# Two block norms of a transformer kernel: four product groups per new tile, and eight kept squares added behind the last low part

## The chip, the cores and the metric

One core of a Trainium2 chip runs the whole program. The metric is the device time of one execution in microseconds (us), median over the runs. Five engines matter: PE (TensorE, matrix products into the eight banks of PSUM), DVE (VectorE), ACT (ScalarE), POOL (GpSimd) and the queue SP, which issues the transfers of weights.

## The reference, cut to what matters

The program is a first block (a mixer of three branches, then a convolutional feed-forward), a second model of two layers (a "fox" attention and a latent attention, each with a feed-forward), on 512 tokens of 1024 channels in float32. The two places that the change touches both have this form:

```
x = x + rmsnorm(y, g_post)          # y: the output projection before it
h = rmsnorm(x, g_pre);  h @ w       # w: ffn_w_up, or the fox projection
rmsnorm(x, g) = x * rsqrt(mean(x*x) + eps) * g
```

## The kernel before

Activations lie transposed, a tile being 128 channels by 512 tokens; 1024 channels are eight tiles (KD = 8). Every float32 product is made of three: high part times high part, high weight times low part, low weight times high part (`split_mm`, lines 596 to 600, and lines 668 to 670 where the tokens stand in the rows). So one tile of one group of 128 output columns is three products, called a triple here. ACT rounds weights and activations to the high part; POOL subtracts and so makes the low part of the weights (WLO, line 590), in pieces of 512 columns, and DVE that of the activations.

The weights come in chunks of 1024 columns through a ring of four slots: SP fetches chunk c when the product groups of chunk c - 4 are done (line 559), ACT casts it (`casts`, line 1203), POOL splits it. `casts(n)` stands at fixed places of ACT's order.

The scale of a norm is not applied before the product but behind it: PE multiplies x times its gain (HH, HL), and DVE multiplies the result by RSTD when it empties the bank. So PE may start on a tile before the sum of squares is known. The sum, SUMSQ, is brought across the partitions by a product with ones (`stats`, line 673, or `stats_in_two`, line 678), and ACT takes the root by Ln and Exp (`root`, line 1219).

The two places are the norm before the first feed-forward (site `ffnpre0`, behind `wout`, here the first norm) and that before the fox attention (site `fox`, behind `down0`, here the second norm). At each:

- ACT squares the projection's tiles (`fb_square`, line 1245), for the last one directly from PSUM, behind `early_table`, which loads the table for Ln.
- PE runs `stats_in_two` and 24 products that are thrown away (`keep_clock(24)`, line 685).
- DVE runs `post_norm` (line 2026). For each tile j: `scaled` (FB times gain and RSTD), `added` (X plus FB), `lo_tile` (HL, once ACT has made HH), and `add_square`, which adds ACT's square to SUMSQ. The loop is written so that tile j+1 is added and j+2 scaled between the low part of j and its square.
- ACT runs for each tile `h_tile` (line 1238): HH, then the square of X into one of two slots of SQ. The square waits until the one two before has been added.
- PE takes the new tiles. First norm (lines 958 to 962): four groups, `gate0.0`, `val0.0`, `gate0.1`, `val0.1` (UP0_HEAD), whose weights share four chunks, two tiles of each group in a chunk. The order is by chunk, then by group, then by the two tiles. `stats` stands in the last chunk behind the second group, so four triples follow it. Second norm (lines 1009 to 1016): four groups of 128 tokens each (`fv0.0` to `fv0.3`), again by chunk, then group, then tile, and `stats` behind all of them; then `foxf`, then `by_token_scale`, which turns RSTD into columns, then `fv1`.

Each PE instruction of these groups waits for the low part of its own tile (`by_tile`). ACT casts the fourth head chunk behind tile 1 at the first norm (line 1430) and behind tile 2 at the second (line 1467), and the chunk after the head behind tile 7 (lines 1431 and 1468), ahead of `root`. Behind `root` it casts `val0.2` (line 1445).

Of the kernel before, what the change touches and what calls it, by code (L numbers as in the profile page):

```python
# [20 lines left out]
ALU = mybir.AluOpType  # L21
ACT = mybir.ActivationFunctionType
# [6 lines left out]
P = 128  # L29
T = 512  # L30
NT = T // P
D = 1024
KD = D // P
# [53 lines left out]
UP0_HEAD = ("gate0.0", "val0.0", "gate0.1", "val0.1")  # L87
# [145 lines left out]
def on_chip_model(nc, xT, weights, params, consts, masks16, masks8, gate_up, pool_w, rope, resets, outT):  # L233
    with ExitStack() as ctx:
# [27 lines left out]
        X = keep("X", [P, KD, T])  # L262
# [7 lines left out]
        SUMSQ = keep("SUMSQ", [P, T])  # L270
# [42 lines left out]
        def over(name, shape, tensor_at, dt=F32):  # L313
            return nc.alloc_sbuf_tensor_at(name, shape, dt, offset=tensor_at)
# [42 lines left out]
        fox = Region(arena)  # L357
# [7 lines left out]
        foh_at = fox.at  # L365
# [4 lines left out]

        FZ = nc.alloc_sbuf_tensor_at("FZ", [P, 2, T], F32, offset=foh_at)
        ONES = nc.alloc_sbuf_tensor_at("ONES", [P, T], F32, offset=foh_at + 2 * T * 4)
        CUMH = over("CUMH", [P, T], foh_at + 3 * T * 4, F32R)
        CUML = over("CUML", [P, T], foh_at + 4 * T * 4, F32R)

# [47 lines left out]
        H = (as_tiles(HH), as_tiles(HL))  # L423
# [15 lines left out]
        lin_done, drained = sem("lin_done"), sem("drained")  # L439

        h_hi, h_lo, sq_done, sumsq, cleared = sem("h_hi"), sem("h_lo"), sem("sq_done"), sem("sumsq"), sem("cleared")
# [64 lines left out]
        def tile(t, j):  # L506

            return t[:, bass.ds(j, 1), :].rearrange("p a n -> p (a n)")
# [86 lines left out]
        def _(pe):  # L595
# [15 lines left out]
            def bank_free(name):  # L611
                if PRIOR[name]:
                    pe.wait_ge(drained, PRIOR[name])

            def part(name, at, hi, lo, ready=None, tiles=None):

                c, first, blocks, col = PARTS[name][at]
                begin, end = tiles or (first, first + blocks)
                if begin == 0:
                    bank_free(name)  # L620
                slot, last = c % RING, at == len(PARTS[name]) - 1
                for k in range(begin, end):
                    n = k - first
                    w = slice(col + n * P, col + (n + 1) * P)
                    weights_ready(c, w.stop)
                    if ready:

                        pe.wait_ge(ready[0], ready[1] + k + 1)
                    mm = split_mm(ps[:, BANK[name], :], WHI[:, slot, w], WLO[:, slot, w], hi[k], lo[k],
                                  k == 0, last and n == blocks - 1)  # L630
                if end == first + blocks:
                    mm.then_inc(lin_done, 1)
# [19 lines left out]
                for at in range(len(PARTS[name])):  # L652
                    part(name, at, hi, lo, ready)

            def token_part(name, at, width, hi, lo, last, rows, ready=None):

                if at == 0:
                    bank_free(name)
                c, first, blocks, col = PARTS[name][at]
                slot, per = c % RING, width // P  # L660
                for n, r in enumerate(rows):
                    o, q = ps[:, BANK[name], n * width:(n + 1) * width], slice(r * P, (r + 1) * P)
                    for m in range(blocks // per):
                        k, w = first // per + m, slice(col + m * width, col + (m + 1) * width)
                        weights_ready(c, w.stop)
                        if ready:
                            pe.wait_ge(ready[0], ready[1] + k + 1)
                        pe.matmul(o, hi[k][:, q], WHI[:, slot, w], start=k == 0, stop=False)  # L668
                        pe.matmul(o, lo[k][:, q], WHI[:, slot, w], start=False, stop=False)  # L669
                        mm = pe.matmul(o, hi[k][:, q], WLO[:, slot, w], start=False, stop=k == last - 1)  # L670
                mm.then_inc(lin_done, 1)

            def stats(site, n):

                pe.wait_ge(sumsq, SQ_AT[site] + n + 2)
                pe.matmul(ps[:, 7, :], ones, SUMSQ[:, :], start=True, stop=True).then_inc(stat_done, 1)
# [16 lines left out]
            def by_tile(site):  # L693
                return h_lo, HH_AT[site]
# [259 lines left out]
            def ffn(f):  # L954
                site = f"ffnpre{f}"
                h = H_OF.get(site, H)
                if f == 0:
                    for at in range(4):
                        for n, name in enumerate(UP0_HEAD):
                            if at == 3 and n == 2:  # L960
                                stats(site, 8)
                            part(name, at, *h, by_tile(site))
                for q in range(0 if f else 2, KF):
                    group(f"gate{f}.{q}", *h, by_tile(site) if q == 0 else None)
                    if q == 0:
                        stats(site, 8)
                    group(f"val{f}.{q}", *h)
                for j in range(KD if f < 2 else KD - 1):
                    group(f"down{f}.{j}", *ACTS[f], (acts, 1 + KF * f) if j == 0 else None)
# [38 lines left out]

            for half in range(2):
                for at in range(NT):  # L1010
                    for r in range(NT):
                        token_part(f"fv{half}.{r}", at, 512, *H, KD, (r,), None if half else by_tile("fox"))
                if half == 0:
                    stats("fox", 8)
                    group("foxf", *H)
                    by_token_scale("fox")
# [183 lines left out]
        def _(act):  # L1200
# [26 lines left out]
            def early_table(func):  # L1227
                warmed[0] += 1
                act.activation(WARM[:, :], con("one"), func).then_inc(warm, 1)
                act.wait_ge(warm, warmed[0])  # L1230

            def square(j, slot, source, site):

                act.wait_ge(sumsq, j + (SQ_AT[site] + 1))
                apart()
                act.activation(SQ[:, slot, :], source, ACT.Square).then_inc(sq_done, 1)  # L1236

            def h_tile(j, slot, gain, site, squares=True):

                apart()  # L1240
                act.activation(H_OF.get(site, H)[0][j], tile(X, j), ACT.Copy, scale=par(gain, j)).then_inc(h_hi, 1)
                if squares:
                    square(j, slot, tile(X, j), site)

            def fb_square(stage, j, site):

                if j < KD - 1:
                    product(f"{stage}.{j}")
                    square(j, j % 2, tile(FB, j), site)
                else:  # L1250
                    early_table(ACT.Ln)
                    act.wait_ge(lin_done, DONE[f"{stage}.{j}"])
                    square(j, j % 2, ps[:, BANK[f"{stage}.{j}"], :], site)

# [170 lines left out]
            root("mixpost", D, RSTD)  # L1425
            for j in range(KD):
                act.wait_ge(x_done, j + 1)
                h_tile(j, j % 2, "ffnpre0", "ffnpre0")
                if j == 1:
                    casts(chunk_of("gate0.0"))  # L1430
            casts(chunk_of("gate0.2"))
# [30 lines left out]
            root("ffnpost", D, RSTD)  # L1462
            for j in range(KD):
                act.wait_ge(x_done, j + (KD + 1))
                h_tile(j, j % 2, "fox", "fox")
                if j == 2:
                    casts(chunk_of("fv0.0"))
            casts(chunk_of("foxf"))
# [198 lines left out]
        def _(dve):  # L1667
# [19 lines left out]
            def add_square(j, slot, site):  # L1687
                dve.wait_ge(sq_done, j + (SQ_AT[site] + 1))

                dve.wait_ge(sumsq, j + (SQ_AT[site] + 2))  # L1690
                dve.tensor_tensor(SUMSQ[:, :], SUMSQ[:, :], SQ[:, slot, :], ALU.add).then_inc(sumsq, 1)  # L1691
# [334 lines left out]
            def post_norm(site, nxt, done):  # L2026

                clear_sum(nxt)
                dve.sem_inc(sumsq, 1)
                scale_known(site)  # L2030

                def scaled(j):
                    stt(tile(FB, j), tile(FB, j), par(site, j), RSTD[:, :], ALU.mult, ALU.mult).then_inc(post_dve, 1)

                def added(j):
                    dve.wait_ge(post_dve, j + (done + 1))
                    dve.tensor_tensor(tile(X, j), tile(X, j), tile(FB, j), ALU.add).then_inc(x_done, 1)

                scaled(0)
                added(0)  # L2040
                scaled(1)
                for j in range(KD):
                    lo_tile(j, nxt, nxt)
                    if j + 1 < KD:
                        added(j + 1)
                    if j + 2 < KD:
                        scaled(j + 2)
                    add_square(j, j % 2, nxt)

            def into_x(stage, site, gain, tiles=KD):  # L2050

# [470 lines left out]
```

## Time and profile before

| | us |
|---|---|
| median of 3 runs | 2198.48 |
| lowest, highest | 2197.4, 2198.51 |
| span of the profiled execution | 2196.6 |

The table holds no time of the profiled execution but its span, from its first to its last instruction; the runs' times also hold what lies around it. Times in rows count from the start of the span. PE's mean granted clock over the span is 0.997 of full speed.

A row of the timeline has an instruction's start and its duration, or, where several alike follow each other, the time that they cover. Consecutive starts tell more than durations, because neighbouring instructions of one engine overlap a little at their ends. The last bracket of a row tells how long the engine was idle before it, and who ended that.

### The profile page before, as it was taken

Reading aid. Unit: us, or ns where it says so; the run is one execution under the profiler, and the core shown is the slowest. Engines: PE = TensorE matmul, PEld = TensorE weight load, DVE = VectorE, ACT = ScalarE, POOL = GpSimd, SP = SyncE. Lnnn points to the kernel's source line nnn. Section 1 sums busy time; section 2 is a strip of 40 time slices with the busy share of each in tenths; the row PEclk is TensorE's granted clock in tenths of the full one; section 3 lists DMA queues with packets and bytes.
Section 4 is the critical chain, followed back from the end, with each engine's and each line's share of the span. In section 5 each row is a group of like instructions: output and inputs, shape, how many; then the busy total and the mean of one; then the engine's idle time right before and its main releaser. Section 6 shows DMA issues by size and latency. Waiting matters only on the chain.

```text
span 2196.6 us, 26113 instructions
## 1 busy us (share of the span) xinstructions
PE 2170.1 (99%) x10388; PEld 1771.0 (81%) x10388; DVE 1201.8 (55%) x1709; ACT 908.1 (41%) x1410; POOL 953.9 (43%) x731
## 2 busy tenths in 40 slices
PE   9999999999999999999999999999999999999998
PEld 6877788878888877777888888887888888888887
DVE  5775324479865126776566661167666425666511
ACT  5224522353443234666533342255544434333323
POOL 5334344545554434321544444544232344544442
PEclk9999999999999999999999999999999999999999
DMA  5222222323333322211333333232111133333332
GB/s 181 78 68 65 75 82 96 106 77 96 96 96 92 98 89 87 68 58 31 114 96 96 96 95 98 95 96 75 56 53 52 60 106 96 96 96 96 94 99 86
DMA packets 58377, 191.76 MB, mean 87 GB/s; under 512 B 6512, under 2 KB 8720, under 8 KB 58256
## 3 DMA queue, kind: packets, MB, share of 16 engines
q1 hardware_dynamic: 58256, 190.09, 27.9%
q8 instruction: 83, 1.36, 0.3%
q14 instruction: 38, 0.31, 0.0%
HBM read 187.96 MB, written 2.10 MB: 87 GB/s over the span
## 4 chain that ended last, share of the span: by engine, by line
PE 92%; DVE 5%; ACT 1%; DMA 1%; issue 1%; SPq 0%; ACTq 0%; POOL 0%; DVEq 0%
PE ps L598 26%; PE ps L600 26%; PE ps L599 26%; PE ps L1111 2%; PE ps L1005 1%; PE ps L668 1%; PE ps L996 1%; PE ps L669 1%; PE ps L670 1%; DMA RAW<-weights 1%; DVE TURNED L1675 1%; PE ps L1060 1%; PE ps L1029 1%; PE ps L726 1%; DVE RT L2264 0%
## 5 line engine op out<-in xcount | busy, mean ns | idle before, releaser
L590 POOL TENSOR_TENSOR WLO<-RAW,WHI 128x512 fp32r<-128x512 f32 (+1 forms) x723 | 951.4, 1342 | 1209.8 <-ACT WHI L1208 1206.7
L1208 ACT ACTIVATE WHI<-RAW 128x1024 fp32r<-128x1024 f32 (+2 forms) x374 | 372.7, 1000 | 661.4 <-DMA RAW<-weights 474.4
L598 PE MATMUL ps<-HH,WHI 128*128 128x512 f32 x1200 | 474.7, 396 | 3.5 <-DVE HL L1678 2.3
L600 PE MATMUL ps<-HH,WLO 128*128 128x512 f32 x1200 | 468.0, 390 | 0.0
L599 PE MATMUL ps<-HL,WHI 128*128 128x512 f32 x1200 | 467.8, 390 | 0.0
L1678 DVE SCALAR_TENSOR_TENSOR CV<-U,PAR,CV 128x512 f32<-128x512 f32 x264 | 287.9, 1109 | 11.2 <-ACT CV L1448 6.1
L598 PEld LDWEIGHTS ps<-HH,WHI 128*128 128x128 f32 x1200 | 225.6, 188 | 57.5 <-issue 5.3
L599 PEld LDWEIGHTS ps<-HL,WHI 128*128 128x128 f32 x1200 | 225.8, 188 | 47.9 <-issue 2.4
L600 PEld LDWEIGHTS ps<-HH,WLO 128*128 128x128 f32 x1200 | 225.6, 188 | 47.6
L598 PE MATMUL ps<-ACTH,WHI 128*128 128x512 f32 (+1 forms) x550 | 209.5, 381 | 0.0
L599 PE MATMUL ps<-ACTL,WHI 128*128 128x512 f32 (+1 forms) x550 | 209.3, 381 | 0.0
L600 PE MATMUL ps<-ACTH,WLO 128*128 128x512 f32 (+1 forms) x550 | 209.3, 381 | 0.0
L1675 DVE TENSOR_TENSOR U<-ps,RSTD 128x512 f32<-128x512 f32 x132 | 89.8, 687 | 209.5 <-PE ps L600 191.0
L1448 ACT ACTIVATE CV<-U,PAR 128x512 f32<-128x512 f32 x132 | 106.5, 808 | 103.3 <-DVE U L1675 103.3
L2056 DVE TENSOR_TENSOR X<-X,ps 128x512 f32<-128x512 f32 x31 | 21.2, 685 | 224.8 <-PE ps L600 224.8
L598 PE MATMUL ps<-HUH,WHI 128*128 128x512 f32 x352 | 137.3, 390 | 0.0
L600 PE MATMUL ps<-HUH,WLO 128*128 128x512 f32 x352 | 136.9, 389 | 0.0
L599 PE MATMUL ps<-HUL,WHI 128*128 128x512 f32 x352 | 136.9, 389 | 0.0
L600 PEld LDWEIGHTS ps<-ACTH,WLO 128*128 128x128 f32 x550 | 103.4, 188 | 19.9
L599 PEld LDWEIGHTS ps<-ACTL,WHI 128*128 128x128 f32 x550 | 103.4, 188 | 19.8
L598 PEld LDWEIGHTS ps<-ACTH,WHI 128*128 128x128 f32 x550 | 103.4, 188 | 19.6
L1691 DVE TENSOR_TENSOR SUMSQ<-SUMSQ,SQ 128x512 f32<-128x512 f32 x77 | 71.3, 926 | 21.0 <-ACT SQ L1236 20.6
(336 smaller groups left out, 3258.5 us busy)
## 6 DMA issues: line engine op xcount, KB each, us to landing
RAW<-weights SPq DMA_DIRECT2D x299, 512.0 KB, 3.5
RAW<-weights SPq DMA_DIRECT2D x48, 384.0 KB, 3.0
RAW<-weights SPq DMA_DIRECT2D x29, 256.0 KB, 2.5
outT<-X SPq DMA_DIRECT2D x8, 256.0 KB, 2.2
X<-xT SPq DMA_DIRECT2D x3, 512.0 KB, 9.0
X<-xT SPq DMA_DIRECT2D x2, 256.0 KB, 3.7
RESET<-resets SPq DMA_DIRECT2D x1, 512.0 KB, 9.4
CS<-rope SPq DMA_DIRECT2D x1, 512.0 KB, 3.6
```

The lines of the kernel that those rows point to most:

```text
L590: pool.tensor_tensor(WLO[:, slot, w], RAW[:, slot, w], WHI[:, slot, w].bitcast(F32), ALU.subtract).then_inc(w_lo, 1)
L598: pe.matmul(out, wh, hh, start=first, stop=False)
L599: pe.matmul(out, wh, hl, start=False, stop=False)
L600: return pe.matmul(out, wl, hh, start=False, stop=last)
L668: pe.matmul(o, hi[k][:, q], WHI[:, slot, w], start=k == 0, stop=False)
L669: pe.matmul(o, lo[k][:, q], WHI[:, slot, w], start=False, stop=False)
L1111: mm = pe.matmul(ps[:, 2 + 3 * odd + bank, col:col + length], q_[:, i * P:(i + 1) * P], k_[:, 0:length], start=False, stop=m == len(produc ...
L1208: act.activation(WHI[:, slot, 0:cols], RAW[:, slot, 0:cols], ACT.Copy).then_inc(w_hi, 1)
L1448: act.activation(CV[:, m, :], U[:, m, 2:2 + T], ACT.Identity, bias=par(f"conv{f}", at + 3), scale=par(f"conv{f}", at + 2)).then_inc(tap, 1)
L1675: return dve.tensor_tensor(out, a, b, ALU.mult)
L1678: return dve.scalar_tensor_tensor(out, a, scalar, b, op0, op1)
L1691: dve.tensor_tensor(SUMSQ[:, :], SUMSQ[:, :], SQ[:, slot, :], ALU.add).then_inc(sumsq, 1)
```

## The change

At both norms PE takes each new tile in all four groups before the next tile. At the first norm `stats` moves behind all 32 triples; at the second it stands there already. The eight squares of X each get a buffer of their own, SQALL, over memory that is free at that time, so ACT's square of a tile no longer waits for DVE. DVE leaves `add_square` out of the loop and adds the eight squares behind the low part of tile 7. Besides, the load of the Ln table for the projection's last square moves one tile earlier (`fb_square`).

```diff
+        SQALL = over("SQALL", [P, KD, T], foh_at + KD * T * 4)
...
-            def token_part(name, at, width, hi, lo, last, rows, ready=None):
-
-                if at == 0:
-                    bank_free(name)
+            def token_part(name, at, width, hi, lo, last, rows, ready=None, tiles=None):
+
                 c, first, blocks, col = PARTS[name][at]
                 slot, per = c % RING, width // P
+                begin, end = tiles or (0, blocks // per)
+                if at == 0 and begin == 0:
+                    bank_free(name)
...
-                    for m in range(blocks // per):
+                    for m in range(begin, end):
...
-                mm.then_inc(lin_done, 1)
+                if end == blocks // per:
+                    mm.then_inc(lin_done, 1)
...
                 if f == 0:
-                    for at in range(4):
-                        for n, name in enumerate(UP0_HEAD):
-                            if at == 3 and n == 2:
-                                stats(site, 8)
-                            part(name, at, *h, by_tile(site))
+                    for k in range(KD):
+                        for name in UP0_HEAD:
+                            part(name, k // 2, *h, by_tile(site), (k, k + 1))
+                    stats(site, 8)
...
-                    for r in range(NT):
-                        token_part(f"fv{half}.{r}", at, 512, *H, KD, (r,), None if half else by_tile("fox"))
+                    if half == 0:
+                        for m in range(2):
+                            for r in range(NT):
+                                token_part(f"fv0.{r}", at, 512, *H, KD, (r,), by_tile("fox"), (m, m + 1))
+                    else:
+                        for r in range(NT):
+                            token_part(f"fv1.{r}", at, 512, *H, KD, (r,))
...
+            def kept_square(j):
+
+                apart()
+                act.activation(SQALL[:, j, :], tile(X, j), ACT.Square).then_inc(sq_done, 1)
+
             def fb_square(stage, j, site):
 
                 if j < KD - 1:
                     product(f"{stage}.{j}")
                     square(j, j % 2, tile(FB, j), site)
+                    if j == KD - 2:
+                        early_table(ACT.Ln)
                 else:
-                    early_table(ACT.Ln)
                     act.wait_ge(lin_done, DONE[f"{stage}.{j}"])
...
-                h_tile(j, j % 2, "ffnpre0", "ffnpre0")
+                h_tile(j, j % 2, "ffnpre0", "ffnpre0", False)
+                kept_square(j)
...
-                h_tile(j, j % 2, "fox", "fox")
+                h_tile(j, j % 2, "fox", "fox", False)
+                kept_square(j)
...
                     if j + 2 < KD:
                         scaled(j + 2)
-                    add_square(j, j % 2, nxt)
+                for j in range(KD):
+                    dve.wait_ge(sq_done, j + (SQ_AT[nxt] + 1))
+                    dve.wait_ge(sumsq, j + (SQ_AT[nxt] + 2))
+                    dve.tensor_tensor(SUMSQ[:, :], SUMSQ[:, :], SQALL[:, j, :], ALU.add).then_inc(sumsq, 1)
```

## Rows read from the trace of the kernel before

**Rows 1.** Page, part 1: busy us (share of the span) xinstructions; PEld is its weight load.
```profile
PE 2170.1 (99%) x10388; PEld 1771.0 (81%) x10388; DVE 1201.8 (55%) x1709; ACT 908.1 (41%) x1410; POOL 953.9 (43%) x731
```

**Rows 2.** Waits of PE, 440 to 900 us: who for whom, total, times, longest.
```profile
PE ps L668 <- DVE HL L1678: 3.8, 3, 1.6
PE ps L598 <- DVE HL L1678: 2.3, 2, 1.5
PE ps L683 <- ACT SQ L1236: 0.6, 1, 0.6
```

**Rows 3.** Timeline, first norm, ACT: start, duration, engine, line, operation [idle before <-releaser].
```profile
438.66 1.28 ACT L1229 ACT_TABLE_LOAD   x1
...
440.30 0.60 ACT L1236 ACTIVATE SQ<-ps 128x512 f32<-128x512 f32 x1
...
446.38 0.72 ACT L1241 ACTIVATE HH<-X,PAR 128x512 fp32r<-128x512 f32 x1 [1.63 <-DVE X L2037]
...
448.60 0.72 ACT L1241 ACTIVATE HH<-X,PAR 128x512 fp32r<-128x512 f32 x1 [0.99 <-DVE X L2037]
...
467.04 1.05 ACT L1208 ACTIVATE WHI<-RAW 128x1024 fp32r<-128x1024 f32 x1
```

**Rows 4.** Timeline, first norm, DVE.
```profile
447.13 0.75 DVE L1678 SCALAR_TENSOR_TENSOR HL<-X,PAR,HH 128x512 fp32r<-128x512 f32 x1 [0.21 <-ACT HH L1241]
447.80 0.68 DVE L2037 TENSOR_TENSOR X<-X,FB 128x512 f32<-128x512 f32 x1
448.40 0.75 DVE L1678 SCALAR_TENSOR_TENSOR FB<-FB,PAR,RSTD 128x512 f32<-128x512 f32 x1
449.06 0.68 DVE L1691 TENSOR_TENSOR SUMSQ<-SUMSQ,SQ 128x512 f32<-128x512 f32 x1
449.66 0.74 DVE L1678 SCALAR_TENSOR_TENSOR HL<-X,PAR,HH 128x512 fp32r<-128x512 f32 x1
...
450.93 1.77 DVE L1678 SCALAR_TENSOR_TENSOR FB<-FB,PAR,RSTD 128x512 f32<-128x512 f32 x1
...
454.31 0.74 DVE L1678 SCALAR_TENSOR_TENSOR HL<-X,PAR,HH 128x512 fp32r<-128x512 f32 x1
...
467.31 0.68 DVE L1691 TENSOR_TENSOR SUMSQ<-SUMSQ,SQ 128x512 f32<-128x512 f32 x1
```

**Rows 5.** Timeline, first norm, PE.
```profile
448.03 0.47 PE L598 MATMUL ps<-HH,WHI 128*128 128x512 f32 x1 [0.77 <-DVE HL L1678]
...
457.65 0.48 PE L598 MATMUL ps<-HH,WHI 128*128 128x512 f32 x1
...
470.69 1.02 PE L676 MATMUL ps<-SUMSQ,CON 128*128 128x512 f32 x2
...
474.31 0.39 PE L598 MATMUL ps<-HH,WHI 128*128 128x512 f32 x1
```

**Rows 6.** Timeline, first norm, POOL.
```profile
450.87 2.97 POOL L590 TENSOR_TENSOR WLO<-RAW,WHI 128x512 fp32r<-128x512 f32 x2 [9.66 <-ACT WHI L1208]
468.16 2.54 POOL L590 TENSOR_TENSOR WLO<-RAW,WHI 128x512 fp32r<-128x512 f32 x2 [14.32 <-ACT WHI L1208]
475.40 9.79 POOL L590 TENSOR_TENSOR WLO<-RAW,WHI 128x512 fp32r<-128x512 f32 x6 [4.71 <-ACT WHI L1208]
```

**Rows 7.** Timeline, second norm, DVE.
```profile
818.88 0.75 DVE L1678 SCALAR_TENSOR_TENSOR HL<-X,PAR,HH 128x512 fp32r<-128x512 f32 x1 [0.21 <-ACT HH L1241]
```

**Rows 8.** Timeline, second norm, PE.
```profile
845.23 1.02 PE L676 MATMUL ps<-SUMSQ,CON 128*128 128x512 f32 x2
```

**Rows 9.** Timeline, feed-forward stage, DVE, a step and one that waits for it.
```profile
494.35 0.69 DVE L1675 TENSOR_TENSOR CV<-CV 128x512 f32<-128x512 f32 x1
495.08 0.43 DVE L2023 TENSOR_SCALAR ACTH<-CV 128x512 fp32r<-128x512 f32 x1
```

**Rows 10.** Windows of the first norm: us, busy by engine, PEclk, DMA share, GB/s.
```profile
448.00:451.00 3.00, 1.46 (x5) 0.97 (x6) 3.00 (x6) 2.19 (x3) 0.13 (x1) 1.00 0.00 0
451.00:454.50 3.50, 3.50 (x10) 2.70 (x9) 3.50 (x4) 1.24 (x2) 2.84 (x2) 0.51 0.00 0
```

## The prediction

> **What bounds the kernel now.** I read the page first: PE is busy for 99% of the span [rows 1], so only what shortens PE's work or fills its holes can count. The waits of PE between 440 and 900 us come next, for both norms lie there. They hold all that this change can remove: PE waits for new low parts (HL) 2.3 us at the first norm and 3.8 at the second, and 0.6 for the square of the last projected tile, once [rows 2]. That is 6.7 us or 0.3% of the time. The timelines of the two stretches then tell what would end last once those waits are gone. A measurement of this kernel can tell some 0.2%, 4.4 us, from no change.
>
> **The table load.** At the first norm ACT loads the Ln table at 438.66 and squares only at 440.30 [rows 3], and PE waits 0.6 for that [rows 2]. Moved one tile earlier, the load lies where ACT waits for weights. I take 0.6 gained; bounds 0 and 0.7. At the second norm PE has no such wait [rows 2], so nothing.
>
> **How fast the tiles come.** Before, a tile costs DVE 2.53 (447.13 to 449.66), all of it issue: low part, added, scaled, square [rows 4]. Without the square DVE would need less than the round trip does: low part to added 0.67 [rows 4], added to ACT's HH 0.80 (447.80 to 448.60), HH to low part 0.75 (446.38 to 447.13) [rows 3, 4]: 2.22 a tile.
>
> POOL runs one split in that stretch, 450.87 to 453.84 [rows 6]. While it does, two DVE instructions take 454.31 - 450.93 = 3.38, where the same two took 449.66 - 448.40 = 1.26 before it [rows 4]: a pair of splits costs a DVE that is never idle 2.1. The cast that releases it keeps its place, so it stays; DVE now has 0.3 idle in each tile, so I take 1.5 (bounds 0 and 2.1). The low part of tile 7 then starts at 447.13 + 7 x 2.22 + 1.5 = 464.2, against 466.64 (467.31 - 0.67) [rows 4]. At the second norm: 818.88 [rows 7] + 15.5 + 1.5 = 835.9.
>
> **PE by tile.** A triple takes 0.68 ((470.69 - 457.65) / 19 triples [rows 5]), so four take 2.72, longer than the 2.22 in which a tile comes. PE, which starts at 448.03, is fed from the first tile on but for some 0.2 at the split: its 32 triples end at 448.03 + 21.9 + 0.2 = 470.1. At the second norm PE starts the same 0.9 behind the first low part, at 819.8, and ends at 841.7. The holes go, then. But `stats` now stands behind everything, and it needs the squares.
>
> **The sum, the new end.** The eight adds follow the last low part by 0.67. Each waits for the one before. Such a pair in the feed-forward stage starts 0.73 apart (494.35, 495.08) [rows 9], where independent instructions of that length start 0.60 apart (447.80, 448.40) [rows 4]. The eight take 7 x 0.73 + 0.68 = 5.8.
>
> They do not run alone. ACT casts the next chunk 0.5 behind its last square (467.04) [rows 3], and POOL starts its split 1.1 later, at 468.16, when DVE's last add has just ended at 467.99 [rows 4, 6]. In the changed kernel that cast comes with tile 7, so the same pair of splits falls on the adds. I price it at 1.9, near the 2.1 above; bounds 0 and 2.1.
>
> First norm: 464.2 + 0.67 + 5.8 + 1.9, and 0.1 to PE, gives `stats` at 472.7; PE has stood for 2.6 us. Before, `stats` started at 470.69 and four triples followed it; `gate0.2` started 3.62 later, of which 0.90 is not triples [rows 5]. Now `gate0.2` starts at 472.7 + 0.9 = 473.6 against 474.31: 0.7 gained, with the table load 1.3.
>
> Second norm: 835.9 + 0.67 + 5.8 + 1.9 + 0.1 = 844.4 against 845.23 [rows 8]; all behind it (root, `foxf`, the columns of RSTD) hangs on `stats` as before. Gained 0.8; PE stands 2.7 ahead of it.
>
> **What is late next.** ACT casts `val0.2` only behind the root; its split starts 4.71 behind `stats` (475.40 - 470.69) and a piece takes 1.63 (9.79 / 6) [rows 5, 6]: ready at 6.34. PE wants it at 0.9 + 8 x 0.68 = 6.34. Before, four triples more lay between. I take 0.1, bounds 0 and 0.5. DVE starts on the feed-forward later against PE than before, by 2.7 us in all; it is covered, as the banks of the head are wanted again only behind two whole groups, 10.9 us. SP sees its slots freed earlier, and nothing waits for that. Eight squares on ACT are the same eight as before.
>
> The sum without the clock: 1.3 + 0.8 - 0.1 = 2.0 gained.
>
> A rule bears on the adds. By the Trainium skill (VectorE: DVE Perf Modes, The DRAIN you can't avoid) a semaphore between chained VectorE instructions costs nothing extra, as the flush comes anyway. By that rule the adds would lie as close as independent ones. The rows above speak against it, 0.73 against 0.60.
>
> **The clock.** The granted clock in this stretch fell once: from 451 to 454.5 it was 0.51, the level of 1.2 GHz, behind three microseconds in which PE was busy for 1.46 [rows 10]. At that level half of 3.5 us is lost, 1.7. Before it cost nothing, since PE had to wait for tile 3 anyway. At the second norm PE waited as long and no fall followed, so PE was near the edge. That fall goes away, because PE now has work there. But the two waits for the sum, 2.6 and 2.7 us in one piece, leave PE idler than the row before the fall shows it, if only for a moment, so either may bring a fall or not. Behind `stats` nothing hides one: PE sets the end. I take a fall at one of the two as likeliest, 1.7 lost.
>
> **The forecast.** 2.0 - 1.7 = 0.3 gained. The profiled span, 2196.6, becomes 2196.3; the median lies 1.9 above the span before, and I keep that: 2198.1. In short: the holes between tiles are filled and come back as one hole before `stats`. Chance 0.38.
>
> **Rivals.**
> - No fall: the whole 2.0 stays, 2196.5. For it: the second norm's waits brought none. Chance 0.22.
> - Falls at both: 2.0 - 3.4, 2199.9. Chance 0.17.
> - POOL's split does not meet the adds, or DVE does not feel it: 1.9 comes back at each norm, the waits shrink below 1 us and no fall follows. But PE's own end takes over: `stats` at 470.9 and 842.5. Gains 2.4 + 0.6 + 2.7 = 5.7, with some 0.3 for the first split: 2192.5. Against it: every add has both inputs where the slowed two had theirs [rows 4]. Chance 0.09.
> - The adds lie 0.60 apart (the rule of that page): 7 x 0.13 = 0.9 more at each norm, 3.8 gained, waits of 1.7 that bring no fall, 2194.7. Chance 0.06.
> - Slower: each of the eight adds takes the price of those under the split, 1.69 (3.38 / 2). That is 13.5 against 7.7, 5.8 more at each norm: 2.0 - 11.6, 2208.1. It decides from the third further slowed add at each norm on (0.96 each). Against it: one pair of splits lasts 2.97 [rows 6], and no other chunk is cast ahead of the root. Chance 0.04.
> - The change does not do what it says: an order by tile that the weights hold up. All four chunks are there when the tiles come, so I give it, with all unnamed, 0.04, near no change.
>
> **Range.** From 2194.6, which takes in the closer adds, to 2200.6, both falls with the split's bound and the wait for `val0.2`. Left out are the missed split and the slow adds. Faster by over 0.2% are the missed split and a margin, 0.11; slower by over 0.2% 0.05; the rest 0.84.
>
> **What would show it.** In the changed profile: low parts 2.2 apart but once; no waits of PE for HL beyond the first tile but a few tenths; eight adds 0.73 apart, two or three of them stretched to some 1.7; PE waiting for SUMSQ 2 to 3 us at `stats` at both norms; the square of the last projected tile ready with the product; the clock at 1.2 GHz, if at all, behind one of the two waits and no longer at tile 2. PE without a wait at `stats`, or adds untouched by POOL, would make this wrong, and the time shorter.

## The result: slower by 5.3 us, above the range

The changed kernel takes 2202.74 us in the median of nine runs (2200.03 to 2204.43), the kernel before 2197.45 beside it: 1.0021 times as long, interval 1.0013 to 1.0029. Forecast were 2198.1 and at most 2200.6. The profiled execution took 2204.17 us, with a span of 2202.4.

The page and the waits of PE between 440 and 900 us (who for whom, total, times, longest) answer to [rows 1, 2] of the kernel before:

```profile
span 2202.4 us, 26113 instructions
...
PE 2173.0 (99%) x10388; PEld 1774.7 (81%) x10388; DVE 1207.0 (55%) x1709; ACT 907.9 (41%) x1410; POOL 953.1 (43%) x731
```

```profile
PE ps L679 <- DVE SUMSQ L2066: 6.3, 2, 3.3
PE ps L670 <- DVE HL L1693: 0.8, 1, 0.8
PE ps L599 <- DVE HL L1693: 0.8, 1, 0.8
PE ps L599 <- POOL WLO L591: 0.7, 1, 0.7
```

Of the 6.1 us for low parts the first tile's 0.8 is left at each norm, and the wait for the square is gone. In their place stand 6.3 us for the sum, and 0.7 for low parts of weights in the feed-forward. So PE waits 8.6 us where it waited 6.7, and that explains 1.9 of the 5.3.

DVE at the first norm (start, duration or time covered, [idle before <-releaser]). The adds are shown in overlapping stretches of the same timeline; each row gives the start of its first add:

```profile
445.21 0.75 DVE L1693 SCALAR_TENSOR_TENSOR HL<-X,PAR,HH 128x512 fp32r<-128x512 f32 x1 [0.21 <-ACT HH L1248]
...
447.45 0.75 DVE L1693 SCALAR_TENSOR_TENSOR HL<-X,PAR,HH 128x512 fp32r<-128x512 f32 x1 [0.22 <-ACT HH L1248]
...
449.68 1.49 DVE L1693 SCALAR_TENSOR_TENSOR HL<-X,PAR,HH 128x512 fp32r<-128x512 f32 x1 [0.22 <-ACT HH L1248]
451.09 1.77 DVE L2052 TENSOR_TENSOR X<-X,FB 128x512 f32<-128x512 f32 x1
...
453.75 0.75 DVE L1693 SCALAR_TENSOR_TENSOR HL<-X,PAR,HH 128x512 fp32r<-128x512 f32 x1 [0.21 <-ACT HH L1248]
...
462.68 0.75 DVE L1693 SCALAR_TENSOR_TENSOR HL<-X,PAR,HH 128x512 fp32r<-128x512 f32 x1 [0.87 <-ACT HH L1248]
463.34 8.05 DVE L2066 TENSOR_TENSOR SUMSQ<-SUMSQ,SQALL 128x512 f32<-128x512 f32 x8
...
464.13 2.39 DVE L2066 TENSOR_TENSOR SUMSQ<-SUMSQ,SQALL 128x512 f32<-128x512 f32 x2
...
464.93 3.28 DVE L2066 TENSOR_TENSOR SUMSQ<-SUMSQ,SQALL 128x512 f32<-128x512 f32 x2
...
466.63 1.58 DVE L2066 TENSOR_TENSOR SUMSQ<-SUMSQ,SQALL 128x512 f32<-128x512 f32 x1
...
468.32 2.28 DVE L2066 TENSOR_TENSOR SUMSQ<-SUMSQ,SQALL 128x512 f32<-128x512 f32 x3
```

Low parts come 2.23 apart, but once: across POOL's split 4.07 (449.68 to 453.75). The eight adds cover 8.05 us. Undisturbed ones start 0.80 apart (463.34, 464.13, 464.93). Behind the third and the fourth, which lie under POOL's second pair of splits (464.19, below), the next add starts only after 1.70 and 1.69.

PE at both norms, then ACT at both, then POOL:

```profile
446.11 0.47 PE L599 MATMUL ps<-HH,WHI 128*128 128x512 f32 x1 [0.77 <-DVE HL L1693]
...
471.45 2.08 PE L679 MATMUL ps<-SUMSQ,CON 128*128 128x512 f32 x2 [2.98 <-DVE SUMSQ L2066]
...
846.86 2.07 PE L679 MATMUL ps<-SUMSQ,CON 128*128 128x512 f32 x2 [3.35 <-DVE SUMSQ L2066]
```

```profile
438.39 0.60 ACT L1243 ACTIVATE SQ<-ps 128x512 f32<-128x512 f32 x1 [0.72 <-PE ps L601]
...
473.57 0.69 ACT L1230 ACTIVATE RSTD<-ps,CON 128x512 f32<-128x512 f32 x1 [8.15 <-PE ps L679]
...
848.97 0.69 ACT L1230 ACTIVATE RSTD<-ps,CON 128x512 f32<-128x512 f32 x1 [8.16 <-PE ps L679]
```

```profile
464.19 3.48 POOL L591 TENSOR_TENSOR WLO<-RAW,WHI 128x512 fp32r<-128x512 f32 x2 [11.87 <-ACT WHI L1215]
```

The last square waits for its product and no longer for the table. But `stats` itself takes 2.08 where it took 1.02 [rows 5], and ACT's Ln starts 2.12 behind its start. The windows say why (us, busy of PE, PEld, DVE, ACT, POOL, then PEclk, DMA share, GB/s):

```profile
468.00:471.00 3.00, 0.47 (x3) 0.04 (x1) 2.58 (x5) 0.00 (x0) 0.00 (x0) 0.91 0.42 127
471.00:474.00 3.00, 2.55 (x4) 1.42 (x5) 0.41 (x2) 0.43 (x1) 0.00 (x0) 0.50 0.12 48
474.00:477.50 3.50, 3.50 (x10) 2.69 (x10) 1.27 (x2) 3.47 (x5) 0.28 (x1) 0.53 0.00 0
843.50:846.50 3.00, 0.01 (x1) 0.00 (x0) 2.58 (x5) 0.00 (x0) 0.00 (x0) 0.90 0.58 168
846.50:850.00 3.50, 3.14 (x5) 1.83 (x6) 0.31 (x1) 1.01 (x2) 0.00 (x0) 0.50 0.04 11
850.00:853.00 3.00, 3.00 (x9) 2.36 (x8) 0.00 (x0) 2.99 (x4) 0.37 (x1) 0.55 0.00 0
```

Late in each wait, ahead of `stats`, the granted clock falls to 0.50, the level of 1.2 GHz, and stays there for some us of products. What is missing from 1.00 sums to 3.0 x 0.09 + 3.0 x 0.50 + 3.5 x 0.47 = 3.4 us at the first norm and as much at the second: each fall lasts 6.8 us. The one before lasted 3.5 x 0.49 x 2 = 3.4 [rows 10].

**Where the time goes.** Five points of the trace cut the stretch: DVE's copy of the last projected tile (FB7), `stats` of the first norm (S1), the first copy of `down0`, the last, `stats` of the second norm (S2), and DVE's copy RCOL, which ends the wait for the root. Between the first and last copy of `down0` all fourteen profiles have 105.4 or 105.5. The other steps:

| kernel | FB7 to S1 | S1 to `down0` | `down0` to S2 | S2 to RCOL | sum against before | medians |
|---|---|---|---|---|---|---|
| before | 29.7 | 236.6 | 32.5 | 7.6 | | |
| changed | 32.4 | 237.6 | 32.4 | 10.5 | +5.7 | +5.3 |
| e1 | 30.7 | 236.5 | 30.4 | 7.6 | -1.9 | -2.4 |
| e2 | 32.4 | 239.7 | 32.4 | 7.7 | +5.0 | +4.4 |
| e3 | 32.4 | 236.6 | 32.4 | 7.7 | +1.9 | +1.9 |
| e4 | 29.7 | 236.7 | 32.5 | 7.6 | -0.5 | -0.3 |
| e5 | 30.6 | 235.7 | 30.4 | 7.6 | -2.7 | -2.3 |
| e6 | 29.7 | 236.5 | 32.5 | 7.6 | -0.1 | -0.5 |
| e7 | 32.4 | 235.8 | 32.4 | 7.7 | +1.1 | +1.3 |
| e8 | 32.4 | 236.6 | 32.4 | 7.7 | +1.9 | +1.3 |
| e9 | 27.9 | 236.8 | 30.5 | 7.6 | -4.3 | -4.3 |
| e10 | 32.4 | 236.5 | 32.5 | 7.6 | +2.6 | +3.2 |
| e11 | 32.4 | 236.6 | 32.4 | 7.7 | +1.9 | +2.7 |
| e12 | 32.4 | 236.6 | 32.4 | 9.3 | +3.6 | +3.9 |

(The sum adds the differences of the four steps to -0.7 for the early table load, where a kernel has it: FB7 starts 1.69 behind the product with ones before it in the kernel before, and 1.01 behind it in the changed kernel and in e4; the last column is the kernel's median less that of before in the same runs.)

So the changed kernel loses 2.7 ahead of the first `stats`, 1.0 behind it and 2.9 behind the second, and gains the table load and 0.1. What surprises is the third column. Where PE had done four triples more before `stats`, `down0` comes no sooner behind it.

Timeline rows for that: the first copy of `down0` before, then, of the changed kernel, PE's only wait in the feed-forward, that copy, and RCOL.

```profile
707.33 0.69 DVE L2069 TENSOR_SCALAR FB<-ps 128x512 f32<-128x512 f32 x1 [6.44 <-PE ps L600]
```

```profile
535.91 0.47 PE L599 MATMUL ps<-HH,WHI 128*128 128x512 f32 x1 [0.73 <-POOL WLO L591]
...
709.02 0.69 DVE L2087 TENSOR_SCALAR FB<-ps 128x512 f32<-128x512 f32 x1 [7.41 <-PE ps L601]
...
857.35 0.16 DVE L1752 COPY RCOL<-ps 128x4 f32<-128x4 f32 x1 [10.54 <-PE ps L707]
```

### The profile page after: what moved, and what is told of

Read it like the earlier page. It is cut to its first block, busy times and chain, and to the rows that moved or that the text cites. A ratio compares the mean times of both kernels' runs of the same rounds, so it can differ in the third digit from the quotient of the medians.

```text
span 2202.4 us, 26113 instructions
## 1 busy us (share of the span) xinstructions
PE 2173.0 (99%) x10388; PEld 1774.7 (81%) x10388; DVE 1207.0 (55%) x1709; ACT 907.9 (41%) x1410; POOL 953.1 (43%) x731
## 3 DMA queue, kind: packets, MB, share of 16 engines
q1 hardware_dynamic: 58256, 190.09, 27.9%
## 4 chain that ended last, share of the span: by engine, by line
PE 87%; DVE 8%; ACT 2%; DMA 1%; issue 1%; ACTq 0%; POOL 0%; SPq 0%; DVEq 0%
PE ps L599 25%; PE ps L601 25%; PE ps L600 25%; PE ps L1118 2%; PE ps L1007 1%; DVE CV L1693 1%; PE ps L998 1%; DVE TURNED L1690 1%; PE ps L670 1%; PE ps L671 1%; PE ps L672 1%; PE ps L1067 1%; DMA RAW<-weights 1%; PE ps L1036 1%; DVE SUMSQ L2066 1%
## 5 line engine op out<-in xcount | busy, mean ns | idle before, releaser
L1693 DVE SCALAR_TENSOR_TENSOR CV<-U,PAR,CV 128x512 f32<-128x512 f32 x264 | 288.9, 1113 | 10.5 <-ACT CV L1462 5.5
L1467 ACT ACTIVATE CV<-CV 128x512 f32<-128x512 f32 x66 | 41.8, 634 | 95.9 <-DVE CV L1693 95.9
```

The lines of the kernel that those rows point to most:

```text
L1467: act.activation(CV[:, 0, :], CV[:, 0, :], func).then_inc(act_done, 1)
L1693: return dve.scalar_tensor_tensor(out, a, scalar, b, op0, op1)
```

## The experiments

At first only one reading stood, here the **PE reading**: behind the first `stats` PE sets the end, as the prediction had it, and the loss is a late sum and dearer falls of the clock. When e1 and e3 missed, the **supply reading** was formed: the feed-forward's weights hang on `stats` (root, then ACT's casts at fixed places behind it, then POOL's splits), so a later `stats` moves the whole feed-forward, whatever PE has done. e1 to e4 ran first, then e5 to e8, then e9 to e12, each set beside its own runs of the kernel before. Where a quoted expectation calls a theory by a letter, it is one of that time, with its numbers beside it; E, the last, is the supply reading together with the falls. All kernels do the whole computation.

**e1: the adds back in the loop.** The order by tile and the kept squares stay.

```diff
-                for j in range(KD):
                     dve.wait_ge(sq_done, j + (SQ_AT[nxt] + 1))
                     dve.wait_ge(sumsq, j + (SQ_AT[nxt] + 2))
                     dve.tensor_tensor(SUMSQ[:, :], SUMSQ[:, :], SQALL[:, j, :], ALU.add).then_inc(sumsq, 1)
```

> The changed kernel, but DVE adds each square inside the loop again, behind the scaling of tile j+2, from the eight kept squares. PE's order by tile stays. Theory A (the eight adds behind the last low part make PE stand at stats, and that wait makes the granted clock fall to half on both sides of it): a tile comes every 2.53 us, still less than the 2.72 of four triples, the sum is ready about 1.3 us behind the last low part, PE has no wait at stats, no fall there, stats starts some 3 us before where it did in the kernel before at each norm; 2190 to 2192 us, 6 to 7 below before. Theory B (PE's order by tile itself costs, by its switches between banks and weights): still slower than before, 2199 or more.

Measured: 2194.96 against 2197.33, ratio 0.999 (0.9981 to 0.9998). It is faster, but 3 us above what was expected. PE does not wait for the sum, and two waits for POOL are new:

```profile
525.77 0.47 PE L599 MATMUL ps<-HH,WHI 128*128 128x512 f32 x1 [1.31 <-POOL WLO L591]
...
532.38 0.47 PE L599 MATMUL ps<-HH,WHI 128*128 128x512 f32 x1 [0.90 <-POOL WLO L591]
```

PE waits 2.2 us in the feed-forward for low parts of weights, a wait that the kernel before did not have [rows 2]. Most of the 2.7 us of the four triples that no longer stand behind `stats` is given back there.

**e2: PE's old order at both norms,** adds behind as in the change. The edit puts the loops of the diff's minus lines back.

> The changed kernel with PE's old order at both norms (by chunk, by group, by two tiles; four triples behind stats at the first norm), and the kept squares added behind the last low part. Theory A: PE stands 2.5 to 3.3 us at stats at both norms and the clock falls behind it as in the changed kernel; the four triples at the first norm now lie behind the sum, so this is as slow as the changed kernel or up to 2.7 us slower: 2202 to 2206. Theory B (the order costs): back near before, 2197.

Measured: 2201.75 against 2197.33, ratio 1.0021 (1.0012 to 1.003), as slow as the changed kernel. Without PE's new order most of the loss stays (4.4 of 5.3), so it comes with the adds behind the last low part. Here the four triples do follow `stats`, at half clock, and `down0` comes 3.0 late instead of 1.0. At the second norm the expectation missed: PE had run slower among the tiles (granted clock 0.81 and 0.62 in the 3 us from 822 and from 825), waited only 0.2 for the sum, and no fall followed (RCOL 7.7 behind `stats`).

**e3: the waits filled.** Fourteen products that are thrown away, ahead of both `stats`.

```diff
+                    keep_clock(14)
                     stats(site, 8)
```

> The changed kernel with 14 products that are thrown away (3.0 us) in front of stats at both norms, so that PE works where it stood. Theory A: stats starts within 0.3 us of where it does in the changed kernel, but no fall of the clock follows, and the 3.4 us lost at each norm at the lower clock, and the 1 us that stats and its wait take longer at it, come back: 2194 to 2197, that is 6 to 8 below the changed kernel. If the late sum alone costs (theory C: the clock is beside the point): within 1 us of the changed kernel, 2202 to 2203.

Measured: 2199.19 against 2197.33, ratio 1.0007 (0.9998 to 1.0016). PE at the first norm:

```profile
468.44 3.19 PE L691 MATMUL ps<-M 128*128 128x512 bf16 x14
471.61 1.13 PE L679 MATMUL ps<-SUMSQ,CON 128*128 128x512 f32 x2
```

In the feed-forward it waits 2.2 us for POOL, as e1 does. It came out between its two expectations. Against the kernel before, the changed kernel lost 5.3 and this one 1.9: with the falls gone, 3.4 us come back, but where the prediction's own sum without the clock had it 2.0 ahead, the kernel is 1.9 behind. The PE reading had no room for that.

**e4: the early table load alone,** in the kernel before.

```diff
                     square(j, j % 2, tile(FB, j), site)
+                    if j == KD - 2:
+                        early_table(ACT.Ln)
                 else:
-                    early_table(ACT.Ln)
```

> The kernel before with the Ln table loaded one tile earlier, nothing else. The wait of PE for the last square at the first norm, 0.6 us, goes: 2196.8, 0.6 to 0.7 below before, hardly to be told from it. A change of the clock behind the first norm could add up to 1.7 us either way.

Measured: 2197.05 against 2197.33, ratio 1.0 (0.9992 to 1.0009). In the trace the square waits for its product and PE's wait for it is gone; the median can't show 0.7.

**e5, e6, e7: casts earlier.** ACT's places for casts move up by one chunk in two groups of the feed-forward, in e1 (e5), in before (e6) and in e3 (e7).

```diff
-                            casts(chunk_of(name) + 3 if f or q > 4 else
-                                  chunk_of("gate0.2") + 2 * q + m + (0, 2, 2, 1, 0)[q])
+                            casts(chunk_of(name) + 3 if f or q > 5 else
+                                  chunk_of("gate0.2") + 2 * q + m + (0, 2, 2, 1, 1, 0)[q])
```

> The kernel with the adds in the loop, and in the first feed-forward the weights of two chunks cast one ACT step earlier (offsets 0, 2, 2, 1, 1, 0 where it has 0, 2, 2, 1, 0). Theory D (the first norm's gain is eaten in the feed-forward: PE runs ahead there of a supply whose casts stand at fixed places of ACT's order, and waits 2.2 us for POOL's low parts): those waits go and the whole kernel is 1.7 to 2.6 us faster than the one with the adds in the loop, 2192.3 to 2193.3, 4 to 5 below before. If the waits are not what holds it: the same as that kernel, 2195.

> The kernel before with those earlier casts alone. PE has no wait for a low part in that feed-forward before, so nothing is to be gained: within 0.5 us of before, 2197. A loss would mean that the earlier casts hold up ACT (they may wait for their transfers).

> The changed kernel with the filler in front of stats and the earlier casts. Theory D: the two waits for the low parts of weights, 2.2 us, go: 2196.6 to 2197.5, 2 us below the kernel with the filler alone. What is left of the changed kernel is then the late sum at both norms, even with before, and the table load, 0.7 gained.

Measured: 2195.09, 2196.84 and 2198.68 against 2197.37, ratios 0.9988 (0.9979 to 0.9997), 0.9999 (0.999 to 1.0008) and 1.0006 (0.9997 to 1.0015). e6 came out as expected, e5 and e7 missed: the waits for POOL shrink only from 2.2 to 1.4, for they move to the chunks that the edit doesn't reach. By its median e5 came out where its expectation put the other case, 2195. In the traces 0.8 of the 2.2 is given back, in the third column of the table; the medians of e1 and e5 don't show it. The traces speak for the supply reading all the same: an edit of ACT's order alone, PE's order untouched, moves `down0` against `stats`, and in before, which has no such waits, by 0.2 at most.

**e8: half the filler,** `keep_clock(7)` in e3's places, to see whether shorter waits bring a fall.

> The changed kernel with 7 thrown-away products (1.5 us) in front of stats, so that PE still stands some 1.5 us at both norms. If what it takes for the fall is a wait as long as that of the changed kernel (3.0 and 3.3 us): no fall behind either, as with the full filler, 2199.2. If a wait of 1.5 us is enough: as the changed kernel, 2202 to 2203; falls at some of the runs would lie between.

Measured: 2198.68 against 2197.37, ratio 1.0007 (0.9998 to 1.0016), as with the whole filler. `stats` of both norms:

```profile
470.69 1.12 PE L679 MATMUL ps<-SUMSQ,CON 128*128 128x512 f32 x2 [1.48 <-DVE SUMSQ L2068]
...
845.12 1.13 PE L679 MATMUL ps<-SUMSQ,CON 128*128 128x512 f32 x2 [1.81 <-DVE SUMSQ L2068]
```

Waits of 1.5 and 1.8 us brought no fall here, and `stats` ran at full speed.

**e10: the kernel before with `stats` behind all 32 triples** and nothing else: the step on which the two readings differ most.

```diff
-                            if at == 3 and n == 2:
-                                stats(site, 8)
                             part(name, at, *h, by_tile(site))
+                    stats(site, 8)
```

> The kernel before with stats at the first norm moved behind all 32 triples, nothing else; no sum is late and PE has the same work. Theory E: stats 2.7 us later, the down tiles too: 2200.0. My reading in the prediction (PE sets the end, root and casts are covered by two groups of 10.9 us): within 0.5 us of before, 2197.4.

Measured: 2200.3 against 2197.14, ratio 1.0015 (1.0007 to 1.0024). Its `stats` and its waits of PE in the feed-forward:

```profile
473.14 1.02 PE L676 MATMUL ps<-SUMSQ,CON 128*128 128x512 f32 x2
```

```profile
PE ps L598 <- POOL WLO L590: 2.2, 2, 1.3
```

PE does the same products as before, its waits for tiles at the first norm are those of e4 and e6 (3.7 us), and it never waits for the sum, yet the kernel loses about 3 us. So the supply reading holds: `stats` later by four triples is the feed-forward later by four triples.

The timelines also show through what. First e10, then the kernel before:

```profile
476.86 1.29 DVE L1674 TENSOR_TENSOR U<-ps,RSTD 128x512 f32<-128x512 f32 x2 [9.12 <-ACT RSTD L1224]
...
534.00 1.06 ACT L1207 ACTIVATE WHI<-RAW 128x1024 fp32r<-128x1024 f32 x1 [4.66 <-DVE ACTL L2023]
535.14 2.98 POOL L590 TENSOR_TENSOR WLO<-RAW,WHI 128x512 fp32r<-128x512 f32 x2 [3.64 <-ACT WHI L1207]
536.56 0.47 PE L598 MATMUL ps<-HH,WHI 128*128 128x512 f32 x1 [0.93 <-POOL WLO L590]
```

```profile
474.41 1.29 DVE L1675 TENSOR_TENSOR U<-ps,RSTD 128x512 f32<-128x512 f32 x2 [6.40 <-ACT RSTD L1225]
...
531.63 1.06 ACT L1208 ACTIVATE WHI<-RAW 128x1024 fp32r<-128x1024 f32 x1 [4.68 <-DVE ACTL L2024]
532.77 1.30 POOL L590 TENSOR_TENSOR WLO<-RAW,WHI 128x512 fp32r<-128x512 f32 x1 [3.63 <-ACT WHI L1208]
534.22 0.47 PE L598 MATMUL ps<-HH,WHI 128*128 128x512 f32 x1
```

DVE can empty the first banks of the feed-forward only with RSTD. From there on it takes group after group (U, the convolution, ACTL), is busy 52.0 of the 56.1 us up to 533.0, and up to 572 (before) or 574 (e10) waits for ACT alone and never for PE. ACT's next cast waits for DVE's ACTL, and POOL for the cast. So the whole chain keeps its distance from the root: in e10 DVE starts 2.45 later and this cast comes 2.37 later. And in the kernel before PE takes that chunk 0.15 behind the end of POOL's piece (532.77 + 1.30 against 534.22), so the chain had no slack there, and no wait of PE that would have told it.

**e9: and the other way.** e1 with `stats` ahead of the last tile's four triples, one tile earlier than in any other kernel.

```diff
                     for k in range(KD):
+                        if k == KD - 1:
+                            stats(site, 8)
                         for name in UP0_HEAD:
                             part(name, k // 2, *h, by_tile(site), (k, k + 1))
-                    stats(site, 8)
```

> The kernel with the adds in the loop, and stats at the first norm ahead of the last tile's four triples (the sum is ready by then). Theory E (the feed-forward behind the first norm runs off stats: root, casts and POOL's splits follow it, and from stats to the first down tile it is 236.5 us whatever PE has done ahead): stats comes 2.7 us earlier, 28 instead of 30.7 behind the first norm's last projected tile, and the down tiles come with it until PE's own products bound them, 2.0 to 2.6 us earlier; 2192.4 to 2193.2. If stats were covered by PE's products (my reading in the prediction): as the kernel with the adds in the loop, 2195.0.

Measured: 2192.8 (2189.62 to 2194.33) against 2197.14, ratio 0.9979 (0.9971 to 0.9988): 4.3 us faster than before, where the changed kernel was 5.3 slower. It is the best version here. `stats` stands 27.9 behind FB7 and doesn't wait, and these are its waits of PE from 440 to 900:

```profile
PE ps L599 <- DVE HL L1694: 2.3, 2, 1.5
PE ps L670 <- DVE HL L1694: 2.1, 2, 1.3
PE ps L999 <- DVE FP L2115: 0.4, 1, 0.4
```

No wait for POOL is left, though the casts are where they were.

**e11, e12: the filler at one norm only,** the second (e11) and the first (e12), to price the two falls.

> The changed kernel with the 14 thrown-away products ahead of stats at the second norm alone. There the fall of the clock costs its full price, 2.8 us between stats and the columns of RSTD: that comes back, 2199.8 to 2200.2.

> The changed kernel with the 14 thrown-away products ahead of stats at the first norm alone. Theory E: PE, if it is not slowed, only waits longer for POOL (2.2 us instead of 0.7), so the fall there costs only 1 us: 2201.5 to 2202. If the fall there costs what it costs at the second norm: 2199.5 to 2200.

Measured: 2199.87 and 2201.07 against 2197.14, ratios 1.0013 (1.0004 to 1.0022) and 1.0017 (1.0008 to 1.0026). e11 is where it was expected, e12 0.4 under its range. Their unfilled `stats`, e11's at the first norm with the window behind it, then e12's at the second with two:

```profile
470.10 1.12 PE L679 MATMUL ps<-SUMSQ,CON 128*128 128x512 f32 x2 [3.01 <-DVE SUMSQ L2067]
```

```profile
470.00:473.50 3.50, 3.40 (x13) 2.51 (x14) 0.06 (x2) 2.21 (x3) 0.00 (x0) 1.00 0.00 0
```

```profile
846.07 1.17 PE L679 MATMUL ps<-SUMSQ,CON 128*128 128x512 f32 x2 [3.34 <-DVE SUMSQ L2067]
```

```profile
846.00:849.50 3.50, 3.43 (x8) 2.47 (x9) 0.02 (x1) 2.19 (x3) 0.00 (x0) 0.65 0.00 0
849.50:853.00 3.50, 3.50 (x15) 2.77 (x15) 0.00 (x0) 3.26 (x4) 2.06 (x2) 0.87 0.00 0
```

The 3.0 us wait, which brought a long fall in the changed kernel's profile, brought none here, and the 3.3 us wait one of half the length (3.5 x 0.35 + 3.5 x 0.13 = 1.7 missing) that started only behind `stats`. So at the first norm Ln follows 1.16 behind `stats` and not 2.12, and RCOL 9.3 and not 10.5.

## Why the prediction was wrong

Against the forecast gain of 0.3 stands a loss of 5.3: 5.6 us. (The forecast's own terms give 2198.2 and not 2198.1, 2196.3 + 1.9; nothing hangs on that 0.1.) The sum without the clock was 3.9 too good (2.0 gained forecast, 1.9 lost in e3), the clock 1.7 too cheap (1.7 forecast, 3.4 between the losses of e3 and of the changed kernel).

**Right: the holes go and come back as one.** Low parts come 2.23 apart (2.22 forecast), no wait for HL is left beyond the first tile, and PE stands for the sum at both norms. The table load gave 0.7 (0.6).

**The failed step: four triples credited at the first norm.** The prediction put `stats` 2.0 later (472.7 against 470.69) and called the result 0.7 gained, because `gate0.2` no longer had four triples ahead of it. That is true of `gate0.2` and of nothing behind it. The prediction's section on what is late next looked at three followers: `val0.2`, whose split it found ready to the hundredth (6.34 against 6.34), DVE's banks, and SP. It took the tie at `val0.2` for a cost of 0.1, and called DVE's later start covered, because the banks of the head are wanted again only behind two whole groups. The banks were covered; the casts were not. ACT casts the later chunks only behind DVE's results of earlier groups, DVE starts on these only with the root, and POOL splits only what is cast, so all of it hangs on `stats`; PE met two of these chunks before they were ready. The tie was the sign. From S1 to `down0` it is 236.5 to 236.7 us in before, e1, e3, e4, e6, e8, e10, e11 and e12, whether four triples follow `stats` (before, e4, e6) or not. In e9, where they follow a `stats` 1.8 earlier than before's, it is 236.8, and PE waits for nothing there. e10 shows it alone (+3.2 where this step has no loss: the four triples only change sides). What is 2.7 at S1 is 2.7 at `down0`.

**Sizes in the same sum.** `stats` stands 32.4 behind FB7, and the forecast had it 472.7 - 441.0 = 31.7; at the second norm 32.4 and 844.4 - 812.75 = 31.65. Of these 0.7 at each norm, 0.36 is the first pair of splits, which costs DVE 17.47 - 7 x 2.23 = 1.86 (445.21 to 462.68) and not 1.5. The rest is in the adds: 0.80 apart and not 0.73, half a microsecond over seven, less 0.1 because POOL's split cost them 0.90 + 0.89 = 1.8 and not 1.9. Together 1.4; with 2.7 that makes 4.1, less 0.1 for the table and 0.1 for `val0.2`, the 3.9 above.

On the adds the prediction weighed a rule of the Trainium skill (VectorE: DVE Perf Modes, The DRAIN you can't avoid), by which the semaphores of a chain cost nothing. The adds did not lie as close as the prediction drew from that: 0.80 apart in the chain, 0.60 for independent instructions [rows 4], more clearly than the rows of before had it. No run here separates the semaphore from the dependence, so which of them costs the 0.2 is not shown. By the Trainium skill (GPSIMD Engine Reference, Key points) POOL contends with VectorE instructions that have two inputs in SBUF. The trace agrees, and it has the price: 0.9 for each add under a split.

**The clock.** The prediction took one fall of 3.4 us at 1.7. In the changed kernel's profile there were two of 6.8 us. At the second norm the fall costs 10.5 - 7.6 = 2.9: Ln comes 1.06 later because `stats` itself runs at half speed, and the products behind it run slow up to RCOL. At the first norm it costs only 1.0 (237.6 against 236.6), for the supply starts later by just those 1.07 of Ln, and what PE loses beyond that it would have spent waiting for POOL: 0.7 of such waits against 2.2 in e3. So the term for the clock was too small twice over: in the length of a fall, and in the delay of the root, which it did not have. The two-sided chance ("either may bring a fall or not") was right: e11 had none at the first norm, e12 a short one at the second. The nine runs of the changed kernel fit this: with a mean clock of 0.998 the run takes 2200.03, at 0.997 2200.82 to 2201.35, at 0.996 2202.74 to 2204.43, at 0.995 2203.52 and 2204.17.

**The rivals.** Both falls (2199.9) had the right mechanism and lay 2.8 under the median, by the step above. The missed split, the closer adds and the slow adds are each refuted by the adds' rows. The slower side had been given to one mechanism, adds that all take POOL's price; the supply behind `stats`, on which the loss hung, was no rival at all.

**Open.** Whether the adds would be free of POOL's split if it came elsewhere was not tried. That a late `stats` delays the feed-forward is shown, and the timelines show the chain in between; a run with DVE's work in it made shorter was not made. What brings a fall of the clock, and how long it lasts, stays open. Each kernel was profiled once. Ahead of FB7 the profiles differ by up to 3.7 us (437.28 to 441.02), and behind RCOL the changed kernel's loses another 1.3 us (the spans differ by 5.8, RCOL by 4.53); the first isn't the change's, for e5 and e9 run the same program up to FB7 and copy it at 437.72 and 441.02; nor, as it seems, is the second: that stretch takes 1343.2 to 1345.6 in the fourteen profiles, and the longest is e6's, whose program there is that of before.

## What to carry to other kernels

When a step that a whole supply chain waits for (here the sum for the root, behind which DVE works through the groups, ACT casts and POOL splits) is moved, follow that chain and not only the engine that is 99% busy: an instruction moved from behind it to ahead of it is no gain, if the chain has no slack. A tie between a supplier and PE in the sum, as at `val0.2`, should be read as no slack and be followed further: here PE met the late chunks some 55 us behind `stats`. And of work that can be done in the loop or behind it, here only the last piece belonged behind: e1 and e9 keep the change's order by tile, take the adds back into the loop, put `stats` ahead of work that doesn't need it, and gain where the change lost.

## What the runs showed of the hardware

- The same wait of PE for about 3 us gave no fall of the granted clock (e11), a fall of 3.4 us (e12, 3.3 us) or one of 6.8 us (changed kernel, 3.0 and 3.3; e2, 3.7). At `stats`, waits of 1.5 and 1.8 gave none (e8). But shorter waits between tiles, 0.8 and then 1.3 to 1.6 gave a fall of 3.4 us in three profiles (the kernel before at the first norm [rows 5, 10], e2 and e10 at the second) and none in others (e4 and e6 at the first, the kernel before at the second). What decides it and what sets the length wasn't found; in the changed kernel's two long falls `stats` already ran at half speed (2.08 and 2.07 us against 1.12 and 1.17).
- A fall delays the engines that wait for PE too: ACT's Ln starts 2.12 behind the start of `stats` instead of 1.16 (e11, after the same wait).
- A pair of splits on POOL takes 3.48 us under the adds against 2.54 alone [rows 6], and costs DVE 1.8 or 1.9, whether DVE is always busy (the adds) or has 0.2 idle per tile (the loop). Those idle times cover hardly any of it.
